# Three first blocks computed by rows, tile by tile, and turned back; masked scores added before their product

## The chip, the cores and the metric

The kernel runs on one core of one Trainium2 chip, as one launch. The metric is the device time of one execution in microseconds. The program keeps five engines busy, each with its own queue that it works off in order: TensorE (PE, matmuls and transposes, its weight loads shown as PEld), VectorE (DVE), ScalarE (ACT), GpSimd (POOL) and the queue that issues most DMAs (SP). They wait for one another by semaphores only.

## What is computed

256 tokens of 1024 values pass through two blocks, in float32. Cut to what the change touches:

```python
def mixer(h, ...):                              # first block: convolution half and gated linear attention half
    ...
    o_f = gla_chunked(qh, kh, vh, af)           # forward; chunks of 64 tokens
    o_b = flip(gla_chunked(flip(qh), flip(kh), flip(vh), flip(ab)))
    o = o_f + o_b                               # in each: where(mask, scores, 0) @ v  +  q_in @ state
    ...
def conv_mlp(h, w_up, conv_w, w_down):
    u = dwconv3(h @ w_up, conv_w)               # width-3 convolution over tokens, 2 x 2816 columns
    gate, val = jnp.split(u, 2, axis=-1)
    return (jax.nn.silu(gate) * val) @ w_down
def first_block(x, ...):
    x = x + rmsnorm(mixer(rmsnorm(x, g0), ...) , g1)
    x = x + rmsnorm(conv_mlp(rmsnorm(x, g2), ...), g3)
def second_block(x, ...):                       # i = 0: fox + stick-breaking attention, then swiglu; i = 1: windows, experts
    x = layer_norm(ALPHA * x + fox_sb_mixer(x, w_in, b_f, w_out), ...)
    x = layer_norm(ALPHA * x + swiglu(x, w_gate_up, w_down), ...)
    x = x + sigmoid(x @ w_ple_gate) * (p @ w_ple_proj)
```

## The kernel before

Tokens lie in two tiles of 128 (t = 0, 1). Every large matrix product is made of float32r matmuls in three parts: high part of the operand by high part of the weights, high by low, low by high. Weights come in chunks of 1 MB (128 x 2048 values: four 128-row slices of 512 columns) through a ring of four slots. For each chunk SP loads `w_raw`, ACT rounds it to `w_hi`, DVE subtracts to get `w_lo` (`split_chunk`), and PE uses both. Chunks are numbered through the program: `w_in` has 0 to 12, `w_out` 13 to 16, `w_up` begins at 17. SP may load into a slot when DVE is done with the low part of its last chunk, ACT may round when PE is done with it. A block of 512 output columns takes two chunks.

The order is written out by hand for each engine; `round_to(c)` on ACT and DVE means "round (split) all chunks below c now", and everything behind it in that engine's program waits for it.

A block is computed in one of two shapes. By rows (`rows_chunk`): the tokens are the stationary side, the weights stream 512 wide, and the result has tokens on the partitions; one block is 2 tiles x 8 slices x 3 parts = 48 matmuls. By columns (`cols_chunk`, `products_t`): the weights are stationary, both token tiles stream 256 wide, and the result has columns on the partitions, as the convolution over tokens, the attention's keys and the next product need it; one block is 96 matmuls.

Ahead of a product, a norm ends tile by tile on DVE (`rms_before`, `normalize`, which add to `t_source`). PE transposes the tile (`turn_tile`, eight 128x128 transposes into PSUM banks 4 to 7, called `scr`), ACT rounds the result to `xt_hi` (`turned`), DVE makes `xt_lo` (`turned`). In `operand` PE does this for both tiles, with matmuls of no use (`keep_warm`) between, and the first block by columns starts when both tiles' high parts are there.

The change touches four places. In order of time: the masked scores `st` of the linear attention (two directions, each multiplied by v on PE); the seam from `w_out` to `w_up` (operand 2); from `w_down` to `ab_in` (operand 3); from `ab_out` to `ffn_up` (operand 5). The two up projections consist of pairs of blocks, gate and value, which PE runs in a loop of five trips (`split_loop`, `up`) while ACT and DVE have the same trips written out.

Of the kernel before, what the change touches and what calls it, by code (L numbers as in the profile page):

```python
# [14 lines left out]
ALU = mybir.AluOpType  # L15
# [101 lines left out]
def build(nc, a, out, upto="end"):  # L117
# [27 lines left out]
    with ExitStack() as ctx:  # L145
# [129 lines left out]
        scr = psum[:, 4:8, :]  # L275

# [375 lines left out]
        def _(act):  # L652
# [108 lines left out]

            act.dma_start(gain[:, 0, :], a["norm_mix_pre"][0:1, :].broadcast_to([P, D])).then_inc(S("first_gain"), 16)
# [68 lines left out]
            for t in range(NT):  # L831
                square_x(t, y, lambda t: act.wait_ge(S("x_tile"), t + 1))
                root_tile(t)
            for j in range(2):
                turned(2, j)


            def up_conv(blocks, r):
# [4 lines left out]
                def middle_tap(h, u, bb):  # L843
                    for k in range(nc_):
                        ch = h * KF + 4 * j + k
                        i = copy(u[:, k, :], acc_t(bb % 2, k), scale=cw[:, 1, ch:ch + 1])
# [86 lines left out]
            if "ab_in" in live:  # L933
# [5 lines left out]
                turned_block(ks_b, ks_t)  # L939
# [28 lines left out]
            if "ab_out" in live:  # L968
                pace("ab_out")
                root_tile(0)  # L970
                turned(5, 0)
                root_tile(1)

            def up_gated(blocks, r):
# [3 lines left out]
                wait_used(act, cv)  # L978
                if j:
                    act.wait_ge(S("h_ready"), KP + j)  # L980
                copy(ug[:, 0:nc_, :], acc_tall(bg % 2, nc_), ACT.Silu).then_inc(S(f"acc_free{bg % 2}"), 1)
# [8 lines left out]
            if "ffn_up" in live:  # L990
                for j in range(1, 4):
# [215 lines left out]
        def _(dve):  # L1207
# [15 lines left out]

            def turned(m, j, n=1):
# [51 lines left out]
            def rms_after(i, name, done):  # L1276
# [8 lines left out]
                round_to(c1 + len(p1_) + 2)  # L1285
# [36 lines left out]
            def follow_norm(name, i, between=None):  # L1322
# [7 lines left out]
                round_to(c1 + len(p1_) + 2)  # L1330
                for t in range(NT):
# [6 lines left out]
                    normalize(t, i, x)  # L1338
                dve.sem_inc(S("gain_used"), 2)
# [73 lines left out]
            round_to(13)  # L1413
            wait_used(dve, gb_b[1] + len(gb_b[4]))
# [53 lines left out]
            def up_conv(blocks, r):  # L1468
# [3 lines left out]
                def outer_taps(h, u, bb):  # L1472
                    dve.wait_ge(S("tap_mid"), 2 * j + h + 1)
                    for tap in (0, 2):
                        o, s = (slice(1, SEQ), slice(0, SEQ - 1)) if tap == 0 else (slice(0, SEQ - 1), slice(1, SEQ))
                        for k in range(nc_):
                            ch = h * KF + 4 * j + k
                            STT(u[:, k, o], acc_t(bb % 2, k)[:, s], cw[:, tap, ch:ch + 1], u[:, k, o], ALU.mult, ALU.add)
                        dve.drain()
                    dve.sem_inc(S(f"acc_free{bb % 2}"), 1)  # L1480

                round_to(cv + 2)
# [18 lines left out]
            if "w_up" in live:  # L1501
                dve.wait_ge(S("cw_turned"), 1)
                spare = 2 * (phase["w_out"][0][0] % 2)
                dve.tensor_copy(cw[:].rearrange("p j k -> p (j k)"), psum[:, spare, 0:3 * 2 * KF]).then_inc(S("cw_ready"), 1)
                operand(2)
# [165 lines left out]
            if "ab_out" in live:  # L1671
                follow_norm("ab_out", 4)

            def up_gated(blocks, r):
# [3 lines left out]
                wait_evacuated(dve, bg)  # L1678
# [11 lines left out]
            if "ffn_up" in live:  # L1690
                operand(5)
# [380 lines left out]
        def _(pe):  # L2072
# [40 lines left out]

            def wait_acc(bb, r=0):
# [245 lines left out]
            pe.wait_ge(S("state_ready"), 1)  # L2360
            for t in range(NT):
# [33 lines left out]
            rows_chunk(out_b[0], 1, yh, yl)  # L2395
            last_rows("w_out", yh, yl)


            def up(blocks, r, m=2):
# [533 lines left out]
```

## Time and profile before

| | |
|---|---|
| three runs | 1809.41, 1809.52, 1811.39 us (median 1809.52) |
| profiled execution, own time | 1811.62 us |
| its span, first to last instruction | 1809.9 us |
| PE busy | 1777.9 us, 98% of the span |
| DVE, ACT, POOL busy | 1373.5, 1099.0, 69.8 us |
| mean granted clock of PE | 0.995 of full speed |

A profile gives for every instruction its engine, its line in the program, its start and how long it took. The busy share of PE counts matmuls of no use as well, so it alone does not say how much of the span is needed. The timeline shows instructions in order of time; in brackets stands how long the engine had been idle before, and whose event ended that. "DVEq" is DVE's sequencer, here the signal that follows a drain. Matmuls overlap: each lasts longer than the distance to the next one, so a stretch is read from starts to starts.

### The profile page before, as it was taken

Reading aid. Unit: us, or ns where it says so; the run is one execution under the profiler, and the core shown is the slowest. Engines: PE = TensorE matmul, PEld = TensorE weight load, DVE = VectorE, ACT = ScalarE, POOL = GpSimd, SP = SyncE. Lnnn points to the kernel's source line nnn. Section 1 sums busy time; section 2 is a strip of 40 time slices with the busy share of each in tenths; the row PEclk is TensorE's granted clock in tenths of the full one; section 3 lists DMA queues with packets and bytes.
Section 4 is the critical chain, followed back from the end, with each engine's and each line's share of the span. In section 5 each row is a group of like instructions: output and inputs, shape, how many; then the busy total and the mean of one; then the engine's idle time right before and its main releaser. Section 6 shows DMA issues by size and latency. Waiting matters only on the chain.

```text
span 1809.9 us, 23787 instructions
## 1 busy us (share of the span) xinstructions
PE 1777.9 (98%) x9653; PEld 1493.8 (83%) x9660; DVE 1373.5 (76%) x1224; ACT 1099.0 (61%) x976; POOL 69.8 (4%) x95
## 2 busy tenths in 40 slices
PE   8999999999999999999999999999999999999997
PEld 6979998887899877778788888888888888888886
DVE  4766785468655565789988888898888888888986
ACT  5545554374344345376676676767767767777763
POOL 2200000200000001000000000000000000000100
PEclk8999999999999999999999999999999999999999
DMA  7444556433555553279999999999999999999991
GB/s 261 164 170 152 186 171 224 153 119 122 183 183 185 184 195 139 71 261 382 333 396 375 344 398 358 368 389 338 392 386 340 399 354 365 395 354 380 403 347 62
DMA packets 250470, 496.75 MB, mean 274 GB/s; under 512 B 10630, under 2 KB 15818, under 8 KB 250368
## 3 DMA queue, kind: packets, MB, share of 16 engines
q1 hardware_dynamic: 244992, 477.30, 72.8%
q0 software_dynamic: 4944, 16.50, 2.5%
q10 hardware_dynamic: 432, 1.57, 0.2%
q8 instruction: 66, 1.08, 0.2%
q14 instruction: 36, 0.29, 0.0%
HBM read 489.56 MB, written 5.78 MB: 274 GB/s over the span
## 4 chain that ended last, share of the span: by engine, by line
PE 91%; DVE 5%; issue 1%; DVEq 1%; ACT 1%; DMA 0%; ACTq 0%; SPq 0%
PE psum L2784 17%; PE psum L2786 16%; PE psum L2785 16%; PE psum L2089 5%; PE psum L2184 5%; PE psum L2186 5%; PE psum L2187 5%; PE psum L2090 5%; PE psum L2091 5%; PE psum L2207 3%; DVE w_lo L1802 2%; PE psum L2169 1%; PE psum L2165 1%; PE psum L2167 1%; DVE w_lo L1216 1%
## 5 line engine op out<-in xcount | busy, mean ns | idle before, releaser
L658 ACT ACTIVATE w_hi<-w_raw 128x2048 fp32r<-128x2048 f32 (+1 forms) x357 | 641.9, 1835 | 97.3 <-PE psum L2091 57.8
L1802 DVE TENSOR_TENSOR w_lo<-w_raw,w_hi 128x2048 fp32r<-128x2048 f32 (+1 forms) x236 | 506.9, 2187 | 72.7 <-ACT w_hi L658 72.5
L2784 PE MATMUL psum<-w_hi,xg_hi 128*128 128x512 f32 x892 | 356.3, 399 | 1.1 <-DVE w_lo L1802 1.1
L1216 DVE TENSOR_TENSOR w_lo<-w_raw,w_hi 128x2048 fp32r<-128x2048 f32 (+2 forms) x121 | 266.3, 2229 | 114.2 <-ACT w_hi L658 111.9
L2786 PE MATMUL psum<-w_hi,xg_lo 128*128 128x512 f32 x892 | 352.3, 395 | 0.0
L2785 PE MATMUL psum<-w_lo,xg_hi 128*128 128x512 f32 x892 | 352.0, 395 | 0.0
L1802 DVE TENSOR_TENSOR w_lo<-raw_more,w_hi 128x2048 fp32r<-128x2048 f32 (+1 forms) x116 | 250.1, 2195 | 35.6 <-ACT w_hi L658 35.3
L658 ACT ACTIVATE w_hi<-raw_more 128x2048 fp32r<-128x2048 f32 (+1 forms) x118 | 210.6, 1823 | 17.4 <-PE psum L2786 12.8
L2184 PE MATMUL psum<-xt_hi,w_hi 128*128 128x256 f32 (+2 forms) x768 | 217.9, 284 | 0.0
L2186 PE MATMUL psum<-xt_lo,w_hi 128*128 128x256 f32 (+2 forms) x768 | 217.1, 283 | 0.0
L2187 PE MATMUL psum<-xt_hi,w_lo 128*128 128x256 f32 (+2 forms) x768 | 217.1, 283 | 0.0
L2786 PEld LDWEIGHTS psum<-w_hi,xg_lo 128*128 128x128 f32 x892 | 167.8, 188 | 39.7
L2784 PEld LDWEIGHTS psum<-w_hi,xg_hi 128*128 128x128 f32 x892 | 167.9, 188 | 39.6 <-DVE w_lo L1802 2.0
L2785 PEld LDWEIGHTS psum<-w_lo,xg_hi 128*128 128x128 f32 x892 | 168.0, 188 | 37.6
L2784 PE MATMUL psum<-w_hi,mh_hi 128*128 128x512 f32 x448 | 178.2, 398 | 0.5 <-DVE w_lo L1802 0.5
L2786 PE MATMUL psum<-w_hi,mh_lo 128*128 128x512 f32 x448 | 176.9, 395 | 0.0
L2785 PE MATMUL psum<-w_lo,mh_hi 128*128 128x512 f32 x448 | 176.8, 395 | 0.0
L2184 PEld LDWEIGHTS psum<-xt_hi,w_hi 128*128 128x128 f32 (+2 forms) x768 | 143.8, 187 | 1.3 <-issue 0.8
L2186 PEld LDWEIGHTS psum<-xt_lo,w_hi 128*128 128x128 f32 (+2 forms) x768 | 143.8, 187 | 0.5
L2187 PEld LDWEIGHTS psum<-xt_hi,w_lo 128*128 128x128 f32 (+2 forms) x768 | 143.8, 187 | 0.3
L658 ACT ACTIVATE mg<-psum 128x512 f32<-128x512 f32 x56 | 33.5, 598 | 166.6 <-PE psum L2786 166.6
L2784 PEld LDWEIGHTS psum<-w_hi,mh_hi 128*128 128x128 f32 x448 | 84.3, 188 | 20.2 <-issue 1.1
(439 smaller groups left out, 2260.6 us busy)
## 6 DMA issues: line engine op xcount, KB each, us to landing
w_raw<-in_moe_w_gate_up SPq DMA_DIRECT2D x150, 1024.0 KB, 8.9
raw_more<-in_moe_w_gate_up SPq DMA_DIRECT2D x74, 1024.0 KB, 8.7
w_raw<-in_moe_w_down SPq DMA_DIRECT2D x64, 1024.0 KB, 7.1
raw_more<-in_moe_w_down SPq DMA_DIRECT2D x32, 1024.0 KB, 7.0
w_raw<-in_w_up SPq DMA_DIRECT2D x22, 1024.0 KB, 5.2
w_raw<-in_ffn_w_gate_up SPq DMA_DIRECT2D x22, 1024.0 KB, 5.5
w_raw<-in_w_in SPq DMA_DIRECT2D x12, 1024.0 KB, 5.9
w_raw<-in_ab_w_in SPq DMA_DIRECT2D x12, 1024.0 KB, 5.2
```

Of the source, the lines that this page charges most:

```text
L658: return act.activation(o, i, func, **kw)
L1216: TT(w_lo[:, k % RING, 0:n], raw(slot, n), w_hi[:, k % RING, 0:n].bitcast(F32), ALU.subtract)\
L1802: TT(w_lo[:, at, 0:n], raw(slot, n), w_hi[:, at, 0:n].bitcast(F32), ALU.subtract).then_inc(S("lo_ready"), 1)
L2089: mm(o, hi(k, t), wh, start=(k == ps[0][0]), stop=False)
L2090: mm(o, hi(k, t), wl, start=False, stop=False)
L2091: m = mm(o, lo(k, t), wh, start=False, stop=(k == kmax))
L2184: mm(o, w_hi[:, slot, cols], xt_hi[:, k, :], start=(k == 0 and c_ % 2 == 0), stop=False, skip_group_check=True)
L2186: mm(o, w_hi[:, slot, cols], xt_lo[:, k, :], start=False, stop=False, skip_group_check=True)
L2187: m = mm(o, w_lo[:, slot, cols], xt_hi[:, k, :], start=False, stop=(k == KD - 1), skip_group_check=True)
L2784: mm(o, hi[:, q, :], wh, start=(q == first), stop=False)
L2785: mm(o, hi[:, q, :], wl, start=False, stop=False)
L2786: m = mm(o, lo[:, q, :], wh, start=False, stop=(q == last))
```

## The change

On DVE the two masked score tiles are added to one, so that PE multiplies one of them by v. At the three seams the first block (gate of both up projections, the keys of `ab_in`) is computed by rows, tile 0 first, by a new function `rows_by_tile`: all that needs only tile 0 stands ahead of the transposes of tile 1. Its result is copied to SBUF by ACT, transposed back by PE after half of the next block (`turned_gate`), and taken from there. The useless matmuls at these seams are gone. DVE and ACT interleave the norms of the two tiles with the halves of a low part (`split_half`) and with tile 0's operand. PE's loop over the pairs of the up projections is written out. Cut to its core:

```diff
+        uv_rows = uv[:].rearrange("p k n -> p (k n)").rearrange("p (t n) -> p t n", n=NB)
+        ks_rows = vs
+        turned_gate = scr[:, 0:2, :].rearrange("p b (f n) -> p (b f) n", n=SEQ)
 # ACT
+            def first_gate(block_):
+                wait_used(act, cc + len(ps))
+                for t in range(NT):
+                    i = copy(uv_rows[:, t, :], acc[bb % 2][t])
+                i.then_inc(S(f"acc_free{bb % 2}"), 1)
             for t in squares("w_out"):
                 root_tile(t)
-            for t in range(NT):
+                if t == 1:
+                    turned(2, 0)
+                    turned(2, 1)
                 square_x(t, y, lambda t: act.wait_ge(S("x_tile"), t + 1))
                 root_tile(t)
-            for j in range(2):
-                turned(2, j)
...
                 round_to(cv + 2)
-                wait_used(act, cv)
                 if j == 0:
+                    first_gate(blocks[0])
+                    round_to(cv + 3)
                     act.wait_ge(S("cw_ready"), 1)
+                    act.wait_ge(S("up_turned"), 2)
+                else:
+                    wait_used(act, cv)
                 middle_tap(0, ug, bg)
 # DVE
+            def split_half(h):
+                k, o = me.chunk, slice(h * (CHUNK // 2), (h + 1) * (CHUNK // 2))
+                dve.wait_ge(S("hi_ready"), k + 1)
+                i = TT(w_lo[:, k % RING, o], w_raw[:, k % RING, o], w_hi[:, k % RING, o].bitcast(F32), ALU.subtract)
+                if h:
+                    dve.drain().then_inc(S("lo_ready"), 1)
+                    me.chunk += 1
             round_to(13)
+            dve.drain()
+            TT(st[:, 0], st[:, 0], st[:, 1], ALU.add).then_inc(S("st_ready"), 1)
-            for t in rms_after(1, "w_out", "x_tile"):
-                pass
-            for t in range(NT):
-                rms_before(t, 2)
+            for t in rms_after(1, "w_out", "x_tile", 1, conv_taps):
+                if t == 0:
+                    split_half(0)
+                    rms_before(0, 2)
+                else:
+                    turned(2, 0)
+                    turned(2, 1)
+                    rms_before(1, 2)
+                    split_half(1)
 # follow_norm("ab_out", 4, first_rows, halves=True)
-                round_to(c1 + len(p1_) + 2)
+                round_to(c1 + len(p1_) + (1 if halves else 2))
...
                     normalize(t, i, x)
+                    if halves:
+                        split_half(t)
 # PE
+            def rows_by_tile(bl, m_, src, between=None):
...
+                high(0, 0)
+                high(1, 0)
+                low_weights(0, 0)
+                low_rows(0, 0)
+                low_rows(1, 0)
+                turn_tile(m_, src, 1)
+                if between:
+                    between()
+                low_weights(1, 0, True)
+                high(0, 1)
+                high(1, 1)
+                low_weights(0, 1)
+                low_rows(0, 1).then_inc(S("w_used"), 1)
+                low_weights(1, 1)
+                low_rows(1, 1, True).then_inc(S("w_used"), 1)
-                        for d in range(2):
-                            mm(o[u], st[:, d, u, pair * NT + t, :], p0[:, t, O_V + h * HEAD_V:O_V + (h + 1) * HEAD_V],
-                               start=(d == 0), stop=False)
+                        mm(o[u], st[:, 0, u, pair * NT + t, :], p0[:, t, O_V + h * HEAD_V:O_V + (h + 1) * HEAD_V],
+                           start=True, stop=False)
+            def up_first(name, m_, src, between=None):
+                gate_b, val_b = phase[name][0:2]
+                turn_tile(m_, src, 0)
+                wait_acc(gate_b[0])
+                rows_by_tile(gate_b, m_, src, between)
...
+                wait_acc(val_b[0])
+                cols_chunk(val_b, 0)
+                wait_evacuated(pe, gate_b[0])
+                for k in range(4):
+                    for t in range(NT):
+                        i = turn(turned_gate[:, k, t * P:(t + 1) * P], uv_rows[:, t, k * P:(k + 1) * P])
+                i.then_inc(S("up_turned"), 1)
+                cols_chunk(val_b, 1)
+                for b_ in phase[name][2:]:
+                    products_t(b_, 0)
-                operand(3, x)
-                products_t(ks_b, 0, 3)
-                products_t(qs_b, 0)
+                turn_tile(3, x, 0)
+                wait_acc(ks_b[0])
+                rows_by_tile(ks_b, 3, x)
+                wait_acc(qs_b[0])
+                cols_chunk(qs_b, 0)
...
+                cols_chunk(qs_b, 1)
```

In `rows_by_tile`, `high(i, t)` is chunk i by tile t with both high parts, `low_weights` high operand by low weights, `low_rows` low operand by high weights: four matmuls each. The three small transposes of the convolution's taps (`cw_rows`) move from the seam to the middle of `w_out`.

PE at the seam from `w_out` to `w_up`, before: the taps' transposes (`cw_rows`), both tiles of `y` turned with useless matmuls (`ones_tri`) around them, then the loop over blocks by columns.

```order
L2412 MATMUL psum<-ident,cw_rows 128x44 x3
L2212 MATMUL psum<-ones_tri 128x512 x8
L2207 MATMUL psum<-ident,y 128x128 x8
L2212 MATMUL psum<-ones_tri 128x512 x5
L2207 MATMUL psum<-ident,y 128x128 x8
L2212 MATMUL psum<-ones_tri 128x512 x2
L371 UNCONDITIONAL_BRANCH
L371 ISA
L2153 ISA
L2167 MATMUL psum<-xt_hi,w_hi 128x256
L2169 MATMUL psum<-xt_hi,w_lo 128x256
```

The same place now.

```order
L2310 MATMUL psum<-ident,y 128x128 x8
L2184 MATMUL psum<-w_hi,xt_hi 128x512 x8
L2184 MATMUL psum<-w_lo,xt_hi 128x512 x4
L2184 MATMUL psum<-w_hi,xt_lo 128x512 x8
L2310 MATMUL psum<-ident,y 128x128 x8
L2184 MATMUL psum<-w_lo,xt_hi 128x512 x4
L2184 MATMUL psum<-w_hi,xt_hi 128x512 x8
L2184 MATMUL psum<-w_lo,xt_hi 128x512 x4
L2184 MATMUL psum<-w_hi,xt_lo 128x512 x4
L2184 MATMUL psum<-w_lo,xt_hi 128x512 x4
L2184 MATMUL psum<-w_hi,xt_lo 128x512 x4
L2287 MATMUL psum<-xt_hi,w_hi 128x256
```

Twenty of the block's 48 matmuls now stand between the transposes of tile 0 and those of tile 1, and the 15 useless ones are gone.

DVE at the same seam, before: two low parts of weights, then the second norm of `w_out` for tile 0 (`stat`, `y`, `x`) and tile 1, and only then the norm that makes the operand `y`.

```order
L1216 TENSOR_TENSOR w_lo<-w_raw,w_hi 128x2048 x2
L1288 TENSOR_TENSOR stat<-stat 128x1
L1265 TENSOR_SCALAR stat<-stat 128x1
L1292 TENSOR_TENSOR y<-psum,gain 128x512
L1256 RECIPROCAL stat<-stat 128x1
L1296 SCALAR_TENSOR_TENSOR x<-y,stat,x 128x1024
L1288 TENSOR_TENSOR stat<-stat 128x1
L1265 TENSOR_SCALAR stat<-stat 128x1
L1292 TENSOR_TENSOR y<-psum,gain 128x512
L1256 RECIPROCAL stat<-stat 128x1
L1296 SCALAR_TENSOR_TENSOR x<-y,stat,x 128x1024
L1265 TENSOR_SCALAR stat<-stat 128x1
```

The same place now.

```order
L1245 TENSOR_TENSOR w_lo<-w_raw,w_hi 128x2048
L1328 TENSOR_TENSOR stat<-stat 128x1
L1303 TENSOR_SCALAR stat<-stat 128x1
L1332 TENSOR_TENSOR y<-psum,gain 128x512
L1294 RECIPROCAL stat<-stat 128x1
L1336 SCALAR_TENSOR_TENSOR x<-y,stat,x 128x1024
L1257 TENSOR_TENSOR w_lo<-w_raw,w_hi 128x1024
L1303 TENSOR_SCALAR stat<-stat 128x1
L1294 RECIPROCAL stat<-stat 128x1
L1311 SCALAR_TENSOR_TENSOR y<-x,stat,gain 128x1024
L1328 TENSOR_TENSOR stat<-stat 128x1
L1303 TENSOR_SCALAR stat<-stat 128x1
```

One of the two low parts is split in halves and put behind tile 0's `x`, and tile 0's operand is made before tile 1's second norm begins.

## Rows read from the trace of the kernel before

**Rows 1.** The page's first line

```profile
span 1809.9 us, 23787 instructions
```

**Rows 2.** Timeline, `w_out` to `w_up`: start us, length us, engine, line, instruction [idle before]

```profile
122.80 0.40 PE L2089 MATMUL psum<-w_hi,ya_hi 128*128 128x512 f32 x1
...
125.40 0.15 DVE L1288 TENSOR_TENSOR stat<-stat 128x1 f32<-128x1 f32 x1
...
128.18 0.40 PE L2091 MATMUL psum<-w_hi,xt_lo 128*128 128x512 f32 x1
...
129.35 0.16 DVE L1288 TENSOR_TENSOR stat<-stat 128x1 f32<-128x1 f32 x1 [1.32 <-ACTq L723]
...
132.21 0.15 DVE L1265 TENSOR_SCALAR stat<-stat 128x1 f32<-128x1 f32 x1 [0.22 <-issue]
...
134.27 1.09 PE L2207 MATMUL psum<-ident,y 128*128 128x128 f32 x8 [3.56 <-DVEq L1274]
...
139.07 0.47 PE L2167 MATMUL psum<-xt_hi,w_hi 128*128 128x256 f32 x1
```

**Rows 3.** Windows: us, length, busy us of five engines, granted clock, DMA share, GB/s

```profile
135.00:136.00 1.00, 1.00 (x7) 0.54 (x6) 0.99 (x1) 1.00 (x2) 0.00 (x0) 0.74 0.50 164
136.00:137.00 1.00, 1.00 (x3) 0.38 (x2) 0.79 (x3) 0.05 (x1) 0.29 (x1) 0.50 0.00 0
...
138.00:139.00 1.00, 1.00 (x6) 0.84 (x5) 0.23 (x1) 0.60 (x2) 0.00 (x0) 0.55 0.87 340
```

**Rows 4.** Timeline, `w_down` to `ab_in`

```profile
328.83 1.07 ACT L658 ACTIVATE xt_hi<-psum 128x512 fp32r<-128x512 f32 x2
...
344.09 1.03 ACT L658 ACTIVATE ks_t<-psum 128x1024 f32<-128x1024 f32 x1 [7.72 <-PE psum L2187]
```

**Rows 5.** Timeline, `ab_out` to `ffn_up`

```profile
447.43 4.49 DVE L1216 TENSOR_TENSOR w_lo<-w_raw,w_hi 128x2048 fp32r<-128x2048 f32 x2
...
451.84 0.68 DVE L1304 SCALAR_TENSOR_TENSOR x<-x,psum 128x512 f32<-128x512 f32 x1
...
454.34 0.40 PE L2091 MATMUL psum<-w_hi,xt_lo 128*128 128x512 f32 x1
...
456.74 1.09 PE L2207 MATMUL psum<-ident,x 128*128 128x128 f32 x8 [2.00 <-DVEq L1320]
...
461.85 1.09 PE L2207 MATMUL psum<-ident,x 128*128 128x128 f32 x8 [1.21 <-DVEq L1320]
461.98 2.48 DVE L1228 TENSOR_TENSOR xt_lo<-psum,xt_hi 128x512 fp32r<-128x512 f32 x4 [0.21 <-issue]
...
475.24 1.03 ACT L658 ACTIVATE ug<-psum 128x1024 f32<-128x1024 f32 x1 [5.89 <-PE psum L2187]
```

**Rows 6.** Chain of waits that ended last: start us, us on the chain, what

```profile
91.91 0.89 PE psum L2368 x8
...
93.67 1.09 PE psum L2368 x8
...
108.10 0.87 PE psum L2207 x8
```

**Rows 7.** Timeline, DVE beside the linear attention's products

```profile
85.57 1.22 DVE L1416 TENSOR_TENSOR gct<-gct,psum 128x1024 f32<-128x1024 f32 x1 [1.96 <-POOL gct L560]
...
91.03 1.23 DVE L1434 TENSOR_TENSOR ya_lo<-gct,ya_hi 128x1024 fp32r<-128x1024 f32 x1 [0.21 <-issue]
```

**Rows 8.** Window of 192 matmuls by columns in `w_up`, over a trip's end (162.3)

```profile
143.27:166.31 23.04, 23.04 (x194) 23.04 (x194) 12.67 (x18) 11.02 (x13) 0.00 (x0) 1.00 0.55 183
```

**Rows 9.** Timeline, ACT and DVE behind the first gate block of `w_up`

```profile
150.98 1.57 ACT L658 ACTIVATE ug<-psum,cw 128x256 f32<-128x256 f32 x4 [7.78 <-PE psum L2187]
...
159.31 2.29 DVE L1216 TENSOR_TENSOR w_lo<-w_raw,w_hi 128x2048 fp32r<-128x2048 f32 x1 [0.83 <-ACT w_hi L658]
164.11 3.39 DVE L1478 SCALAR_TENSOR_TENSOR uv<-psum,cw,uv 128x255 f32<-128x255 f32 x8 [2.51 <-ACT uv L658]
...
168.97 2.29 DVE L1216 TENSOR_TENSOR w_lo<-w_raw,w_hi 128x2048 fp32r<-128x2048 f32 x1
```

More of the change, by code:

```diff
@@ L971, in _ @@
                 turned(5, 0)
+                turned(5, 1)
                 root_tile(1)
@@ L990, in _ @@
             if "ffn_up" in live:
-                for j in range(1, 4):
+                for j in range(2, 4):
                     turned(5, j)
@@ L1274, in rms_before, with rms_after @@
                 dve.drain().then_inc(S("t_source"), 2)
-            def rms_after(i, name, done):
+            def rms_after(i, name, done, ahead=2, between=None):
                 (b0, c0, _, _, p0_), (b1, c1, _, _, p1_) = phase[name]
@@ L1284, in rms_after @@
                 dve.drain().then_inc(S(f"acc_free{b0 % 2}"), 1)
[L1285 removed]
+                if between:
+                    between()
+                round_to(c1 + len(p1_) + ahead)
                 for t in range(NT):
@@ L1472, in outer_taps @@
                 def outer_taps(h, u, bb):
+                    first = h == 0 and j == 0
                     dve.wait_ge(S("tap_mid"), 2 * j + h + 1)
@@ L1477, in outer_taps @@
                             ch = h * KF + 4 * j + k
-                            STT(u[:, k, o], acc_t(bb % 2, k)[:, s], cw[:, tap, ch:ch + 1], u[:, k, o], ALU.mult, ALU.add)
+                            src = turned_gate[:, k, s] if first else acc_t(bb % 2, k)[:, s]
+                            STT(u[:, k, o], src, cw[:, tap, ch:ch + 1], u[:, k, o], ALU.mult, ALU.add)
                         dve.drain()
-                    dve.sem_inc(S(f"acc_free{bb % 2}"), 1)
-                round_to(cv + 2)
+                    if not first:
+                        dve.sem_inc(S(f"acc_free{bb % 2}"), 1)
+                round_to(cv + (2 if j else 3))
                 outer_taps(0, ug, bg)
@@ L1501, in _ @@
             if "w_up" in live:
[L1502 to L1505, printed above, removed]
+                for j in range(2, 4):
+                    turned(2, j)
                 split_loop(dve, "w_up", up_conv, me, unroll=True)
@@ L1671, in _, with first_rows @@
             if "ab_out" in live:
-                follow_norm("ab_out", 4)
+                def first_rows():
+                    if "ffn_up" in live:
+                        turned(5, 0)
+                        turned(5, 1)
+                follow_norm("ab_out", 4, first_rows, halves=True)
             def up_gated(blocks, r):
@@ L1690, in _ @@
             if "ffn_up" in live:
-                operand(5)
+                for j in range(2, 4):
+                    turned(5, j)
                 split_p(0)
@@ L2112, in rows_operand_high_first, with part, high, low_weights @@
                 m.then_inc(S("w_used"), 1)
+            def rows_by_tile(bl, m_, src, between=None):
+                bb, cc, n0, n, ps = bl
+                def part(i, t, of, w, last=False):
+                    for k in range(4 * i, 4 * i + 4):
+                        j = mm(acc[bb % 2][t][:, 0:n], of(k, t), w[:, (cc + i) % RING, (k - 4 * i) * n:(k - 4 * i + 1) * n],
+                               start=(k == 0 and of is xh and w is w_hi), stop=(last and k == 4 * i + 3))
+                    return j
+                def high(i, t):
+                    pe.wait_ge(S("hi_ready"), cc + i + 1)
+                    pe.wait_ge(S("xt_hi_ready"), 4 * m_ + 2 * t + i + 1)
+                    part(i, t, xh, w_hi)
+                def low_weights(i, t, last=False):
+                    pe.wait_ge(S("lo_ready"), RING + cc + i + 1)
+                    return part(i, t, xh, w_lo, last)
+                def low_rows(i, t, last=False):
+                    pe.wait_ge(S("xt_ready"), 4 * m_ + 2 * t + i + 1)
+                    return part(i, t, xl, w_hi, last)
+                high(0, 0)
[4 more added lines that the diff above has]
+                turn_tile(m_, src, 1)
+                if between:
+                    between()
+                low_weights(1, 0, True)
[5 more added lines that the diff above has]
+                low_rows(1, 1, True).then_inc(S("w_used"), 1)
             def wait_acc(bb, r=0):
@@ L2572, in _ @@
             if "ffn_up" in live:
-                operand(5, x)
-                turn_p(0)
-                split_loop(pe, "ffn_up", lambda blocks, r: up(blocks, r, 5))
+                up_first("ffn_up", 5, x, lambda: turn_p(0))
             if "ffn_down" in live:
```

60 lines of the change are left out of this document (39 added, 21 removed).

## The prediction, as it was put on record

> **What bounds the kernel now.** I read the page first, then PE's waits, then the timeline around each of the four places. PE is busy for nearly the whole span [rows 1], so a change gains time only where PE waits for something or does work that is not needed; DVE and ACT count only where PE waits for them. The waits named the seams, and the timeline shows what is in them. Between `w_out` and `w_up`, PE issues its last useful matmul at 128.18 and its next at 139.07 [rows 2]: nearly 11 us, of which 16 transposes are needed. It stands still for 3.56 of that, then the granted clock falls to half, the 1.2 GHz level, for about three microseconds [rows 3]. At `ab_out` to `ffn_up`, PE waits 2.00 and 1.21 around the two tiles, with useless matmuls between [rows 5]. In the linear attention the products with `st` come in four groups, 0.89 on the chain for the first and 1.09 for each of the other three [rows 6], and PE waits for nothing there.
>
> **The change part by part.** I carry each place forward on the clock of before, as if the places ahead of it had gained nothing, and add up. A matmul by rows costs (128.18 - 122.80) / 23 = 0.234 us from start to start [rows 2], so a block by rows is 48 x 0.234 = 11.2. By columns 192 take 23.04 [rows 8]: 0.12 each, 5.8 for half a block, 11.5 for a block. The end of a first block I read from the ACT copy that waits for it: 150.98, 344.09 and 475.24 [rows 9, 4, 5]. It trails the last issue by about 0.35 (139.07 + 11.5 against 150.98).
>
> *Masked scores.* Half of 0.89 + 3 x 1.09 goes: 2.1 us. The new addition on DVE is 1024 wide, 1.23 by its nearest row [rows 7]. It stands where DVE was idle for 1.96 until 85.57 waiting for POOL, with a drain before it; the products start at 91.9. Without this cover it would cost at most 1.4 on DVE, and since PE and the chain behind it both start from these products, all that follows moves by the same 2.1.
>
> *`w_out` to `w_up`, until the gate block ends.* The taps' three transposes now stand on PE's path, 0.35 (eight larger ones take 0.87 [rows 6]). Tile 0 of `w_out` is last issued at 122.57, now 122.9. For tile 1 the statistic follows the last issue by 129.35 - 128.18 = 1.17; for tile 0 before it came only at 125.40, because DVE was in the second of two low parts. With one of them put later the statistic comes at 124.1. From there to the finished x is under 132.21 - 129.35 = 2.86, less 0.22 idle: 126.75. Now ACT squares x while nothing hides it: 1.03, as its other 1024-wide copies take, and 0.3 for reading the sum and the hand-over: 128.1. DVE uses this time for half a low part (1.23). From the scalar step to the transposes are 134.27 - 132.21 = 2.06: tile 0 is turned at 130.3, and PE, done at 128.75, waits 1.5. The first rounded half is there 1.3 later (estimate: 0.5 for four transposes, half of 1.03 on ACT, two hand-overs): real matmuls start at 131.6 instead of 139.07. Twenty of them last to 136.3. Meanwhile DVE takes tile 1: statistic 130.2, x 132.85, square 134.2, transposes possible at 136.4. PE waits 0.1, transposes 1.0, waits perhaps 0.3 for the second half of the low part (136.35 + 1.23), and does the other 28: 144.4, with the trail 144.75, against 150.98. That is 6.2.
>
> *`w_down` to `ab_in`.* DVE and ACT do here what they did. The first rounded half is there at 328.83 + half of 1.07, so PE starts at 329.4; tile 1 has long been normalised when PE gets to it. 329.4 + 11.2 + 1.0 for the transposes + 0.35 = 341.95 against 344.09: 2.2.
>
> *`ab_out` to `ffn_up`.* DVE splits one chunk less ahead of tile 0 (4.49 / 2 = 2.25 at 447.43), so tile 0's add moves from 451.84 to 449.6 and its transposes from 456.74 to 454.5, when PE is just done (454.34). Real matmuls start 1.3 later, at 455.95; twenty last to 460.65. On DVE tile 1 follows tile 0 by 461.85 - 456.74 = 5.1, and now has half a low part (1.23) and two of the four low operand pieces (2.48 / 2) in front: 462.1. PE waits 1.4, turns tile 1 and the four blocks of p (1.6), does 28 more: 470.2, with the trail 470.6 against 475.24: 4.7.
>
> *Turned back.* Eight transposes, 0.87 [rows 6], three times: 2.6 lost. The ACT copies to SBUF before them end within half a block by columns (5.8), which hides them.
>
> *The first pair of `w_up`.* Everything ACT does for the gate now starts from the transposes back, half a block later against PE than before. From ACT's first tap to the low part of chunk 22 are 159.31 + 2.29 - 150.98 = 10.6; PE needs it two half blocks after the transposes, 11.5: just in time. The outer taps of the value block then start right behind it instead of at 164.11, and from them to the low part of chunk 23 are 168.97 + 2.29 - 164.11 = 7.15: in all 17.9 from ACT's start, 18.1 from the transposes. PE needs it after 3 half blocks, 17.3: a new wait of 0.8 that stands nowhere before. Behind this low part on DVE are chunk 24 and the next taps; by the same rows both are early by 1.5 or more, so it occurs once. Bounds: 0 to 2. In `ffn_up` the gate needs one ACT instruction instead of taps, and the same sum leaves some 6 us of room.
>
> *PE's loops written out.* I put this at nothing: over a trip's end PE is busy 23.04 of 23.04 us, so no branch costs anything now [rows 8]. The Trainium skill says otherwise in "Runtime: NRT & Kernel Launch", section "Instruction fetch mechanics": instructions are fetched ahead in sequence only, and a taken branch to code outside the fetched pages stalls until its page has come. By that rule writing out eight trip ends would give something on top; the trace does not show a stall, and the sum takes nothing for it.
>
> Sum: 2.1 + 6.2 + 2.2 + 4.7 - 2.6 - 0.8 = 11.8. The profiled execution would go from a span of 1809.9 to 1798.1; its own time, 1811.6, lies 2.1 above the median of the runs, 1809.5, from which I take the same 11.8: **1797.7 us**. What I could not read from the trace are the hand-overs in the new order (bounds: 1.5 each way at the two long seams), the new wait (0 to 2) and the clock (below). With these the case itself reaches from 1795 to 1801.
>
> **Rivals.**
>
> *The clock falls.* The useless matmuls are gone, and PE now waits 1.5, does 1 us of transposes and waits again before the real work. Before, a wait of 3.56 with 8 transposes behind it was followed by half clock [rows 2, 3]. Against it: after a wait of 2.00 the eight transposes took 1.09 like elsewhere [rows 5], and no wait of mine is longer. One fall costs 0.26 + 0.50 + 0.50 + 0.45 = 1.7 us of PE's work at full speed; at the two long seams and `ab_in` up to 5. The time: 1799.5 to 1803.
>
> *Tile 1 is late.* PE's queue holds 28 matmuls, the value block and all else behind the transposes of tile 1. If DVE and ACT get in each other's way there (ACT takes tile 0's rounding between tile 1's root and its square, DVE two pieces of the operand between), the wait is not 0.1 and 1.4 but 3 to 4 at each long seam, and half of the gain is left: about 1803. For it speaks that four hand-overs in a row are new; against it that each of them was laid out above from a measured one.
>
> *The written-out PE code comes too slowly.* 8 blocks of each up projection, 1536 matmuls in all, become straight code. If that code came slower than PE eats it, each would be longer than 0.12. From 11.8 / 1536 = 0.008 on, 6% more, the change is slower than before; at 0.014 the time is 1819. Against it: the blocks of `w_out` are written out and run evenly at 0.234 for a matmul twice as wide, and those of `ab_in` are written out by columns and leave PE no gap.
>
> *It does not do what it says.* If a wait in `rows_by_tile` covers both tiles after all, only masked scores and the missing useless matmuls count: 1804 to 1807.
>
> **How the numbers follow.** My case 0.70; clock 0.12; late tile 1 0.11; not what it says 0.03; slow code 0.04. The range from 1794 to 1803.5 holds the first two and most of the third. What a measurement of this kernel can tell from no change is 0.2%, 3.6 us, so faster means below 1805.9. All of the first three cases and half of the fourth do: 0.94. Same: 0.03; slower: 0.03.
>
> **What would show it.** In the trace of the changed kernel: the `st` group with half its matmuls and about 0.5 long; at `w_up` the first 512-wide matmul some 3 us behind the last of `w_out`, a wait under 0.5 ahead of tile 1, and the ACT copy of the gate 6 us earlier; at `ab_in` 2 us earlier; at `ffn_up` no wait ahead of tile 0 and 1 to 2 us ahead of tile 1. One PE wait of about 0.8 for a low part of weights, in the second value block of `w_up`. A granted clock of 1.00 throughout the seams. I am wrong if the clock falls at a seam, if PE waits over 2.5 for tile 1, if the wait for the low part comes back in later pairs, or if matmuls by columns in the up projections are further apart than 0.121.

## The result, and the profile after

The changed kernel takes 1796.87 us (median; 1796.84 to 1798.10), the kernel before, timed beside it, 1809.47: a ratio of 0.993, 95% interval 0.9912 to 0.9947. Forecast were 1797.7 us and a range of 1794 to 1803.5. The profiled executions took 1811.62 and 1798.10 us. The page's first line, beside the one of before [rows 1]:

```profile
span 1796.4 us, 23383 instructions
```

PE at the three seams, timeline of the changed kernel (start us, length us, engine, line, instruction, idle before and what ended it). L2310 is a transpose, L2184 a matmul by rows.

```profile
128.20 1.09 PE L2310 MATMUL psum<-ident,y 128*128 128x128 f32 x8 [1.15 <-DVEq L1312]
129.63 2.10 PE L2184 MATMUL psum<-w_hi,xt_hi 128*128 128x512 f32 x8 [0.34 <-ACT xt_hi L662]
...
134.37 1.04 PE L2310 MATMUL psum<-ident,y 128*128 128x128 f32 x8
135.60 1.20 PE L2184 MATMUL psum<-w_lo,xt_hi 128*128 128x512 f32 x4 [0.19 <-DVEq L1259]
...
321.54 2.11 PE L2184 MATMUL psum<-w_hi,xt_hi 128*128 128x512 f32 x8 [1.19 <-ACT xt_hi L662]
...
445.23 1.05 PE L2310 MATMUL psum<-ident,x 128*128 128x128 f32 x8
446.62 2.10 PE L2184 MATMUL psum<-w_hi,xt_hi 128*128 128x512 f32 x8 [0.34 <-ACT xt_hi L662]
...
452.67 1.09 PE L2310 MATMUL psum<-ident,x 128*128 128x128 f32 x8 [1.15 <-DVEq L1360]
```

Between `w_out` and `w_up` the first real matmul is issued at 129.63, where before it was at 139.07 [rows 2]; tile 1's transposes at 134.37 wait for nothing. At `ffn_up` tile 0 does not wait, tile 1 waits 1.15. The waits of 3.56, 2.00 and 1.21 before [rows 2, 5] are gone; the longest at the three seams is now the 1.19 of `ab_in`.

Windows of the changed kernel over the same two seams (us, length, busy us of PE, PEld, DVE, ACT, POOL, granted clock, DMA share, GB/s):

```profile
126.00:130.00 4.00, 2.51 (x15) 1.72 (x14) 3.22 (x9) 2.25 (x7) 0.00 (x0) 1.00 0.00 0
130.00:134.00 4.00, 4.00 (x19) 3.26 (x18) 3.50 (x6) 1.35 (x3) 0.00 (x0) 1.00 0.00 0
134.00:138.00 4.00, 3.81 (x21) 2.99 (x20) 2.77 (x5) 2.99 (x4) 1.07 (x2) 1.00 0.25 46
...
448.00:456.00 8.00, 6.85 (x37) 5.42 (x36) 7.30 (x11) 2.84 (x5) 1.64 (x3) 1.00 0.10 19
```

The granted clock is 1.00 throughout, the 2.4 GHz level (in both traces of the changed kernel, and without a break from 20 to 1756 us), where before it was 0.50 for some three microseconds [rows 3].

Beside the short waits at the seams, one wait of PE is new in the changed kernel, and it comes once (waiter, what it waited for: us in total, times, longest):

```profile
PE psum L2287 <- DVE w_lo L1245: 0.7, 1, 0.7
```

**Two pairs of executions.** The two spans of the profiled executions differ by 13.5 us, the medians by 12.6. Both kernels were profiled once more (experiments 11 and 12): spans of 1807.6 and 1795.6, 12.0 apart. The marks of that second pair follow; each mark is the same work in both kernels. The kernel before:

```profile
90.73 1.05 PE L2368 MATMUL psum<-p,st 128*128 128x128 f32 x8
98.57 1.02 ACT L658 ACTIVATE e<-psum 128x1024 f32<-128x1024 f32 x1 [8.00 <-PE psum L2374]
149.99 1.57 ACT L658 ACTIVATE ug<-psum,cw 128x256 f32<-128x256 f32 x4 [7.72 <-PE psum L2187]
321.07 0.58 ACT L658 ACTIVATE psum<-psum 128x512 f32<-128x512 f32 x1 [2.21 <-PE psum L2091]
341.81 1.03 ACT L658 ACTIVATE ks_t<-psum 128x1024 f32<-128x1024 f32 x1 [7.71 <-PE psum L2187]
353.20 1.03 ACT L658 ACTIVATE qs_t<-psum 128x1024 f32<-128x1024 f32 x1 [6.76 <-PE psum L2187]
473.19 1.03 ACT L658 ACTIVATE ug<-psum 128x1024 f32<-128x1024 f32 x1 [5.89 <-PE psum L2187]
484.71 1.22 DVE L1681 TENSOR_TENSOR uv<-ug,psum 128x1024 f32<-128x1024 f32 x1 [4.17 <-PE psum L2187]
```

The changed kernel (its first blocks are copied to `uv` and `vs`):

```profile
91.42 0.61 PE L2471 MATMUL psum<-p,st 128*128 128x128 f32 x4
97.47 1.02 ACT L662 ACTIVATE e<-psum 128x1024 f32<-128x1024 f32 x1 [5.33 <-PE psum L2477]
142.34 1.09 ACT L662 ACTIVATE uv<-psum 128x512 f32<-128x512 f32 x2 [2.75 <-PE psum L2184]
315.28 0.58 ACT L662 ACTIVATE psum<-psum 128x512 f32<-128x512 f32 x1 [2.21 <-PE psum L2155]
333.79 1.09 ACT L662 ACTIVATE vs<-psum 128x512 f32<-128x512 f32 x2 [2.26 <-PE psum L2184]
346.05 1.02 ACT L662 ACTIVATE qs_t<-psum 128x1024 f32<-128x1024 f32 x1 [2.87 <-PE psum L2290]
460.78 1.09 ACT L662 ACTIVATE uv<-psum 128x512 f32<-128x512 f32 x2 [2.30 <-PE psum L2184]
473.24 1.22 DVE L1744 TENSOR_TENSOR uv<-ug,psum 128x1024 f32<-128x1024 f32 x1 [0.69 <-PE psum L2290]
```

Subtract each mark of after from the one of before (-0.69, 1.10, 7.65, 5.79, 8.02, 7.15, 12.41, 11.47); the step from one difference to the next is what the stretch between gained. The first difference is scatter: over the fourteen traces the products with `st` start at 90.1 to 91.8, whatever the kernel.

| stretch, up to | predicted | first pair | second pair |
|---|---|---|---|
| the linear attention's result is read | 2.1 | 1.79 | 1.79 |
| the first gate block of `w_up` is read | 6.2 | 6.54 | 6.55 |
| the end of `w_down` (turned back, new wait) | -1.7 | -0.56 | -1.86 |
| the keys of `ab_in` | 2.2 | 2.22 | 2.23 |
| the queries of `ab_in` (turned back) | -0.9 | -0.87 | -0.87 |
| the gate block of `ffn_up` | 4.7 | 5.05 | 5.26 |
| the first value block of `ffn_up` (turned back) | -0.9 | -0.87 | -0.94 |
| sum | 11.8 | 13.3 | 12.2 |

At the gate block of `ffn_up` the second pair has 0.2 more than the first: in the second trace of the kernel before the clock fell at this seam, too, in the first it did not.

### The profile page after: what moved, and what is told of

It is laid out like the page before. It is cut to its first block, busy times and chain, and to the rows that moved or that the text cites. A ratio compares the mean times of both kernels' runs of the same rounds, so it can differ in the third digit from the quotient of the medians.

```text
span 1796.4 us, 23383 instructions
## 1 busy us (share of the span) xinstructions
PE 1766.9 (98%) x9479; PEld 1482.2 (83%) x9483; DVE 1377.1 (77%) x1227; ACT 1101.7 (61%) x982; POOL 75.1 (4%) x95
## 4 chain that ended last, share of the span: by engine, by line
PE 90%; DVE 6%; issue 1%; ACT 1%; DVEq 1%; DMA 0%; ACTq 0%; SPq 0%
PE psum L2901 17%; PE psum L2903 17%; PE psum L2902 17%; PE psum L2287 6%; PE psum L2290 5%; PE psum L2289 5%; PE psum L2153 5%; PE psum L2155 5%; PE psum L2154 5%; PE psum L2310 3%; DVE w_lo L1866 1%; PE psum L2184 1%; DVE w_lo L1245 1%; DMA w_raw<-in_w_in 0%; DVE x L1357 0%
## 5 line engine op out<-in xcount | busy, mean ns | idle before, releaser
L1245 DVE TENSOR_TENSOR w_lo<-w_raw,w_hi 128x2048 fp32r<-128x2048 f32 (+3 forms) x119 | 262.3, 2230 | 111.9 <-ACT w_hi L662 109.8
L2287 PE MATMUL psum<-xt_hi,w_hi 128*128 128x256 f32 (+2 forms) x880 | 249.1, 283 | 0.7 <-DVE w_lo L1245 0.7
L2290 PE MATMUL psum<-xt_hi,w_lo 128*128 128x256 f32 (+2 forms) x880 | 248.0, 282 | 0.0
L2289 PE MATMUL psum<-xt_lo,w_hi 128*128 128x256 f32 (+2 forms) x880 | 248.0, 282 | 0.0
L662 ACT ACTIVATE w_hi<-raw_more 128x2048 fp32r<-128x2048 f32 (+1 forms) x118 | 210.5, 1824 | 16.1 <-PE psum L2903 12.6
L2287 PEld LDWEIGHTS psum<-xt_hi,w_hi 128*128 128x128 f32 (+2 forms) x880 | 164.5, 187 | 2.4 <-issue 1.7
L2289 PEld LDWEIGHTS psum<-xt_lo,w_hi 128*128 128x128 f32 (+2 forms) x880 | 164.5, 187 | 0.6
L2290 PEld LDWEIGHTS psum<-xt_hi,w_lo 128*128 128x128 f32 (+2 forms) x880 | 164.4, 187 | 0.3
```

Of the source, the lines that this page charges most:

```text
L662: return act.activation(o, i, func, **kw)
L1245: TT(w_lo[:, k % RING, 0:n], raw(slot, n), w_hi[:, k % RING, 0:n].bitcast(F32), ALU.subtract)\
L2287: mm(o, w_hi[:, slot, cols], xt_hi[:, k, :], start=(k == 0 and c_ % 2 == 0), stop=False, skip_group_check=True)
L2289: mm(o, w_hi[:, slot, cols], xt_lo[:, k, :], start=False, stop=False, skip_group_check=True)
L2290: m = mm(o, w_lo[:, slot, cols], xt_hi[:, k, :], start=False, stop=(k == KD - 1), skip_group_check=True)
```

## The experiments

All are timed beside the kernel before, which took 1809.3 to 1810.0 in the median. The question left by the first pair was the third row: 1.1 us too good. In its traces matmuls by columns stand 0.1200 us apart, from start to start, in `w_up` before [rows 8], 0.1187 after, and the change writes PE's loop there out.

**1, the loop written out in the kernel before.**

```diff
-                split_loop(pe, "w_up", up)
+                split_loop(pe, "w_up", up, unroll=True)
```

(and the same for `ffn_up`)

> The kernel before with PE's trips of both up projections written out, nothing else. In the changed kernel the matmuls by columns of w_up stand 0.1187 us apart, 0.1200 before; over the 1056 of w_up that is about 1.3 us that the prediction did not have. Theory A (the loop costs nothing, as predicted; 0.1200 has another cause): 1809.5, w_up still at 0.1200. Theory B (the loop code slows it): 1808.2, w_up at 0.1187.

Measured: 1809.84 against 1809.34, ratio 1.0001 (0.9992 to 1.0011). The time is theory A's, but the distance in `w_up` is 0.1187: neither theory has both.

**5, the loop put back in the changed kernel.**

```diff
-                for b_ in phase[name][2:]:
-                    products_t(b_, 0)
+                trips, bl = LOOPS[name][0] - 1, phase[name][2:]
+                with pe.Fori(0, trips) as r:
+                    for b_ in bl[0:2]:
+                        products_t(b_, r)
...
```

> The changed kernel with PE's trips 2 to 5 of both up projections in a loop again (the first pair stays written out). Theory A (the loop costs nothing): 1796.9, w_up at 0.1187. Theory B (the loop makes 0.1200 in w_up): 768 matmuls x 0.0013 = 1.0 more, 1797.9.

Measured: 1797.32 (1796.93 to 1798.76) and 0.1187 in `w_up` from 150 us on (0.1193 to 0.1198 in the 8 us before). The loop costs nothing to speak of and does not make the distance.

**11 and 12, both kernels unchanged, profiled again.**

> The kernel before, unchanged, in another profiled execution. Theory A (the distance of 0.1200 between matmuls by columns of w_up in the first trace is a property of that execution, since the same loop ran at 0.1187 in two of the experiments): 0.1187 here is possible, w_up then 1.4 shorter. Theory B (it belongs to this kernel, by what stands ahead of w_up): 0.1200 again. Time 1808.5 to 1812 either way.

> The changed kernel, unchanged, in another profiled execution. Theory A: 0.1187 or 0.1200 in w_up, the rest of each seam within 0.1 of the first trace. Theory B: 0.1187 again. Time 1796.8 to 1798.2.

Measured: 1809.34 and 1797.33. The first matmul by columns of `w_up` and the first matmul of `w_down` in the second trace of before:

```profile
138.32 0.36 PE L2167 MATMUL psum<-xt_hi,w_hi 128*128 128x256 f32 x1
...
263.71 0.39 PE L2089 MATMUL psum<-w_hi,ht_hi 128*128 128x512 f32 x1
```

and the latter in its first trace, which answers to 139.07 [rows 2]:

```profile
265.98 0.39 PE L2089 MATMUL psum<-w_hi,ht_hi 128*128 128x512 f32 x1
```

Between the two lie 125.39 us here, 126.91 in the first trace of the same program; experiments 1, 2 and 3 have 125.51, 125.39 and 125.39. So the 0.1200 belonged to the one execution that was profiled first, and some 1.5 us of the first pair's 13.5 are not the change's.

**2, the masked scores alone, in the kernel before.**

```diff
+            dve.drain()
+            TT(st[:, 0], st[:, 0], st[:, 1], ALU.add).then_inc(S("st_ready"), 1)
...
-                        for d in range(2):
-                            mm(o[u], st[:, d, u, pair * NT + t, :], ...
+                        mm(o[u], st[:, 0, u, pair * NT + t, :], ...
```

> The kernel before with the masked scores added on DVE and multiplied once, nothing else. Prediction: 2.1 us less, 1807.4. By the trace of the changed kernel the copy that follows is 1.8 earlier: 1807.7. Rival (the addition on DVE makes something else late, or w_out takes the gain back at its wait for weights): 1809 or more.

Measured: 1807.61 against 1809.34, ratio 0.9988 (0.9978 to 0.9998). From the products to the copy of their result are 6.05 us (90.37 to 96.42) against 7.84 before: 1.79 again, and the medians agree. Its ten executions spread from 1805.2 to 1810.1, and with the granted clock: three at a mean of 0.997 took 1805.2 to 1805.6, seven at 0.994 or 0.995 took 1807.2 to 1810.1. In the profiled one, of the former, the clock stayed at 1.00 between `w_out` and `w_up`, and from tile 0's transposes to the first matmul by columns are 3.53 us, against 4.80 in the first trace of before.

**3, the kernel before without useless matmuls at the seams.**

```diff
-            BEFORE = (0, 10, 8, 0, 18, 0, 4, 0, 18, 0, 24)
-            BETWEEN = (0, 4, 5, 9, 4, 13, 4, 2, 4, 11, 4)
+            BEFORE = (0, 10, 0, 0, 18, 0, 4, 0, 18, 0, 24)
+            BETWEEN = (0, 4, 0, 0, 4, 0, 4, 2, 4, 11, 4)
...
+                if m not in (2, 3, 5):
                     keep_warm(2, 3)
```

> The kernel before without the useless matmuls at the three seams (operands 2, 3 and 5), nothing else. Theory A (they only fill waits): 1809.5, within 0.6. Theory B (without them the clock stays at half for longer behind the seams): up to 3 us more, with windows of granted clock below 1.00 that last beyond the first matmuls by columns. Theory C (w_up runs at 0.1200 because it is entered behind useless matmuls at half clock): 0.1187 in w_up and 1808.2.

Measured: 1813.13 against 1809.34, ratio 1.002 (1.001 to 1.003): theory B, 3.8 for a bound of 3. Windows of its trace at `ab_out` to `ffn_up`, columns as above:

```profile
454.00:456.00 2.00, 1.11 (x5) 1.11 (x6) 1.80 (x3) 0.00 (x0) 0.00 (x0) 0.74 0.64 232
456.00:460.00 4.00, 0.85 (x4) 0.45 (x3) 3.40 (x6) 1.28 (x3) 0.00 (x0) 0.50 0.00 0
460.00:464.00 4.00, 4.00 (x19) 4.00 (x20) 3.18 (x5) 2.33 (x4) 1.82 (x3) 0.50 0.57 198
464.00:466.00 2.00, 2.00 (x14) 2.00 (x14) 0.90 (x2) 2.00 (x2) 0.00 (x0) 0.70 0.77 256
```

PE waits, 2.00 ahead of tile 0 and 3.15 ahead of tile 1 with only transposes between, the clock goes to 0.50, the 1.2 GHz level, and stays there into the block: 19 matmuls and transposes in 4 us, where later windows have 19 in 2. The same is seen at `w_up` (0.50 from 131 to 137). So the useless matmuls paid for themselves before, and the clock rival was no idle fear: the changed kernel leaves them out too. How much of the 3.8 falls at the seams, the traces tell: from the first product with `st` to the first matmul of `ffn_down` are 498.10 here and 496.18 in the second trace of before, 1.9 more, within the bound. Another 2.0 lie far behind, where the code is the same: there the clock is at 0.50 from 1779.5 to 1786 here, from 1768.6 to 1771.9 in that trace of before. Whether the edit has to do with that is not shown. Why does the changed kernel's clock hold?

**4, the changed kernel with both tiles turned first.**

```diff
+                turn_tile(m_, src, 1)
                 high(0, 0)
                 high(1, 0)
                 low_weights(0, 0)
                 low_rows(0, 0)
                 low_rows(1, 0)
-                turn_tile(m_, src, 1)
```

> The changed kernel with tile 1 turned ahead of the whole first block at all three seams, so that no real matmul stands between the tiles. Theory A (the gain of the two long seams is that twenty matmuls of tile 0 lie beside tile 1's norm): each long seam loses 20 x 0.233 = 4.7, ab_in gains up to 1.0 (its 1.19 wait is covered by the second tile's transposes), together 8.4 more than 1796.9: 1805.3; and, since PE then waits with nothing between the tiles, the clock falls as it did without useless matmuls (experiment before this), which adds 1 to 4: 1805 to 1810. Theory B (the order of the tiles does not matter, the gain is the missing useless matmuls): within 1 of 1796.9.

Measured: 1811.65, ratio to before 1.0011 (1.0002 to 1.002): 14.8 lost, the whole gain and more. Its waits (columns as above):

```profile
PE psum L2310 <- DVEq L1360: 6.5, 1, 6.5
PE psum L2310 <- DVEq L1312: 6.2, 2, 5.1
PE psum L2310 <- DVEq L1337: 2.7, 1, 2.7
```

and the clock at `w_up`:

```profile
128.00:132.00 4.00, 0.00 (x0) 0.00 (x0) 3.42 (x8) 1.92 (x5) 0.00 (x0) 0.62 0.00 0
132.00:134.00 2.00, 1.06 (x5) 1.09 (x6) 1.88 (x2) 0.00 (x0) 0.00 (x0) 0.50 0.00 0
134.00:136.00 2.00, 2.00 (x9) 1.77 (x8) 1.25 (x3) 1.68 (x3) 1.07 (x2) 0.56 0.40 45
```

Theory A, but worse than its range, and my expectation for `ab_in` was wrong: tile 1 is not there in time, PE waits 2.7 for its norm. From tile 0's transposes to the first matmul by columns this kernel needs 19.54, 17.26 and 21.71 us at the three seams, the changed one 14.02, 14.34 and 15.40: 14.7 together.

**10, the same with the waits covered by useless matmuls.**

```diff
+                keep_warm({2: 18, 3: 9, 5: 24}[m_])
                 turn_tile(m_, src, 1)
                 high(0, 0)
```

> The kernel with both tiles turned first (1811.7) and useless matmuls between the tiles: 18, 9 and 24 of them at the three seams, 0.22 us each, just shorter than its waits of 5.06, 2.72 and 6.47 there. Theory A (that kernel lost 10.8 by the order and some 4 more because the clock fell behind the uncovered waits): the clock stays at 1.00 at the seams, 1807 to 1808.5. Theory B (the clock costs nothing here, all is the order): 1811.7. Theory C (useless matmuls delay tile 1): above 1812.

Measured: 1807.52 (1806.44 to 1808.10), ratio 0.9989 (0.998 to 0.9999). Windows at `w_up` and `ffn_up`:

```profile
130.00:134.00 4.00, 2.92 (x16) 1.31 (x14) 3.38 (x7) 1.35 (x3) 0.00 (x0) 1.00 0.00 0
...
454.00:458.00 4.00, 2.79 (x14) 1.21 (x13) 3.52 (x7) 0.20 (x1) 0.00 (x0) 1.00 0.00 0
```

Theory A. With cover the clock holds, the three stretches take 18.13, 15.75 and 19.97, and 4.1 us come back by the medians, 4.7 by the three stretches. Of the 14.8 that experiment 4 lost, 4 to 5 were clock and some 10 the order itself. In the changed kernel the twenty real matmuls of tile 0 do both: they fill the wait with work that has to be done, and the clock is held.

**9, `ab_in` by columns in the changed kernel.**

```diff
-                turn_tile(3, x, 0)
-                wait_acc(ks_b[0])
-                rows_by_tile(ks_b, 3, x)
...
+                operand(3, x)
+                products_t(ks_b, 0, 3)
+                products_t(qs_b, 0)
```

> The changed kernel with the seam from w_down to ab_in as before: both tiles turned with useless matmuls between, the keys by columns, no turning back. The prediction's terms for this seam are 2.2 less 0.9: 1.3 more than 1796.9, 1798.2. Rival (the seam gave nothing, and what the trace shows as 2.2 is taken back behind it): 1796.9, within 0.4.

Measured: 1799.17 (1797.41 to 1799.50). In the traces the stretch from the first matmul of `w_down` to tile 0's transposes at `ffn_up` is 188.64 here and 187.26 in the changed kernel: 1.38, the predicted size. The two profiled executions differ by 1.40 as a whole (1799.50 against 1798.10). The medians differ by 2.3; what the other 0.9 is stays open, the four times being 2.1 apart themselves.

**6, chunk 22 rounded earlier in the changed kernel.** Its new wait of 0.7 ends a chain in which DVE stands idle 3.23 us for ACT:

```profile
157.26 2.29 DVE L1245 TENSOR_TENSOR w_lo<-w_raw,w_hi 128x2048 fp32r<-128x2048 f32 x1 [3.23 <-ACT w_hi L662]
```

```diff
                 round_to(cv + 3)
+                if j == 0:
+                    round_to(end + 2)
                 act.wait_ge(S("gate_conv"), j + 1)
```

> The changed kernel with one move on ScalarE: in the first pair of w_up chunk 22 is rounded ahead of the silu of the gate, not behind it. In the trace of the changed kernel VectorE stands idle 3.23 for it, and PE's new wait of 0.73 for chunk 23 is the end of that chain. Theory A (the wait is the late start of the gate's taps, as predicted, and this idle time is where it can be taken out): wait gone, 0.7 less, 1796.2. Theory B (the chain is held by the taps themselves): wait stays, 1796.9.

Measured: 1796.25 (1795.25 to 1796.43); no wait of PE for `w_lo` is left at `w_up`, and DVE, timeline:

```profile
153.30 2.29 DVE L1247 TENSOR_TENSOR w_lo<-w_raw,w_hi 128x2048 fp32r<-128x2048 f32 x1
156.01 3.39 DVE L1537 SCALAR_TENSOR_TENSOR uv<-psum,cw,uv 128x255 f32<-128x255 f32 x8 [0.42 <-ACT uv L662]
```

Theory A: 0.6 less by the medians; from the first matmul by columns of `w_up` to the first matmul of `w_down` are 114.87 us, against 115.76 in the changed kernel, 0.9 less.

**7, the half low part behind tile 1's norm at `ffn_up`.**

```diff
-                    if halves:
-                        split_half(t)
+                    if halves and t:
+                        split_half(0)
+                        split_half(1)
...
-                low_weights(1, 0, True)
+                if m_ != 5:
+                    low_weights(1, 0, True)
                 high(0, 1)
                 high(1, 1)
+                if m_ == 5:
+                    low_weights(1, 0, True)
```

> The changed kernel, at ab_out to ffn_up alone: both halves of the split low part stand behind tile 1's norm on VectorE, and PE multiplies by that low part after tile 1's high parts. Theory A (the wait of 1.15 ahead of tile 1 is the half low part of 1.23 in front of tile 1's norm): wait gone, 1.1 less, 1795.8. Theory B (it only moves the wait to the low part): 0.2 less at most, with a wait of about 1 for the low part.

Measured: 1795.89 (1795.49 to 1796.38). Of the wait of 1.15 ahead of tile 1 this is left:

```profile
PE psum L2314 <- DVEq L1360: 0.2, 1, 0.2
```

and no new one for the low part: theory A, 1.0 less by the medians. From tile 0's transposes to the first matmul by columns are 14.54 here and 15.40 in the changed kernel, 0.9 less. The stretches say more than the medians here: most executions of experiments 6 and 7 have a mean clock of 0.997, the changed kernel 0.996, and in the trace of 7 the clock is at 1.00 from 1757 to 1760, where it is at 0.50 in that of the changed kernel.

**8, both, and `ab_in`'s first tile rounded before tile 1's root.**

```diff
                 for t in squares("w_down"):
+                    if t == 1 and "ab_in" in live:
+                        turned(3, 0)
+                        turned(3, 1)
                     root_tile(t)
```

(DVE's two `turned(3, ...)` move likewise behind tile 0 of `rms_after`; the edits of 6 and 7 are in.)

> The two moves before together, and at w_down to ab_in tile 0's operand is rounded ahead of tile 1's root (its wait of 1.19 on PE is for the rounded half, which stands behind that root on ScalarE). If the three waits are independent: 0.7 + 1.1 + 0.5 = 2.3 less, 1794.6, faster than both kernels. If one of them only moves on: 1795 to 1796.

Measured: 1793.62 (1793.26 to 1795.96), ratio to before 0.9913 (0.9899 to 0.9926). Each of its five times is below each of the changed kernel's (1796.8 to 1798.1), so this version beats both. What is left of its waits:

```profile
PE psum L2193 <- ACT xt_hi L662: 1.4, 3, 0.7
PE psum L2322 <- DVEq L1317: 1.2, 1, 1.2
```

In its trace the three stretches are 114.87 for 115.76, 13.85 for 14.34 and 14.55 for 15.40: 2.2 together, for 2.3 expected, so the three waits are independent. That the medians differ by 3.2 goes with three executions at a mean clock of 0.998 (1793.3 to 1793.6; the two at 0.996 took 1795.2 and 1796.0). Where those three save it wasn't traced.

## Why the prediction was right

*Masked scores.* Right, 1.8 for 2.1 in three traces. A group with half its matmuls now takes 0.53 to 0.64 of PE's time, not half of 0.89 and 1.09 [rows 6].

*`w_out` to `w_up`.* Right, 6.5 for 6.2. The chain ran as laid out, some 2 us earlier in the program's time by then: tile 0 waited 1.15 (forecast 1.5), the first rounded half 0.34, tile 1 nothing (0.1), the half low part 0.19 (0.3). The first matmul by rows stands 9.44 earlier than the first by columns before; 2.0 of that come from what lies ahead of the seam. Of the 6.5, about 1.3 is the half clock that the kernel before lost here: in experiment 2, whose clock stayed at 1.00, the same code took 3.53 for 4.80.

*Turned back.* Right to 0.1: 0.87 and 0.9 where they stand alone.

*The new wait.* Right in place, size and number: 0.73 for 0.8, once, for the low part in the second value block. Experiment 6 shows that the gate's late start was not all of its cause: ACT's order left DVE idle, and the wait could be had for nothing.

*`w_down` to `ab_in`.* The size is right, 2.2, and experiment 9 bears out the net. The premise that tile 1 is long normalised when PE gets to it held, by 3.4 us:

```profile
321.60 1.28 DVE L1336 SCALAR_TENSOR_TENSOR x<-y,stat,x 128x1024 f32<-128x1024 f32 x1
...
326.27 1.04 PE L2310 MATMUL psum<-ident,x 128*128 128x128 f32 x8
```

It holds only because the twenty matmuls stand in front, as experiment 4 showed with its wait of 2.7.

*`ab_out` to `ffn_up`.* Right, 5.05 and 5.26 for 4.7. Tile 0 waits 0, tile 1 1.15 (forecast 1.4).

*Loops written out.* Right at nothing (experiments 1 and 5). The rule of the Trainium skill that was weighed against it ("Runtime: NRT & Kernel Launch", section "Instruction fetch mechanics") would give something on top if the start of a trip lay outside the fetched pages, which no run shows; in these runs a loop of PE's with trips of 192 matmuls costs nothing that can be seen.

*The clock.* Right that it did not fall, but the argument given for it does not hold. The prediction took a wait of 2.00 for harmless, because in its trace the eight transposes behind that wait took 1.09 [rows 5]. In the second trace of the same kernel they take 1.97, and the granted clock is 0.50 from 455 to 457:

```profile
454.47 1.97 PE L2207 MATMUL psum<-ident,x 128*128 128x128 f32 x8 [2.00 <-DVEq L1320]
```

It fell at this seam in experiments 1 and 3 as well, behind the same wait. That it held in the trace that the prediction was read from was chance, and the argument with it. What the runs show in its place: experiment 4 takes the twenty matmuls from between the tiles, PE waits 5.1, 2.7 and 6.5, and the clock falls at all three seams; experiment 10 fills these waits, and it holds. In the changed kernel real work stands there and no wait at a seam is over 1.19. Whether the short waits or the amount of work between them decides is not told apart by any run. The Trainium skill's "TensorE: Matmul & The Clock Gate", section "HAM oscillation — how this bites in real kernels", tells of a clock that falls at waits with little work between them, and regroups the work so that more of it stands between two. Experiments 4 and 10 agree that such waits cost clock: 4.1 us at three seams.

That the first two spans differ by 13.5 and not by 11.8 comes from the trace that the prediction was read from: it held an execution in which `w_up` ran 1.5 us longer than usual. Each term of the sum is a difference of marks on either side of one seam, so this hardly entered it. Two of its steps are off as written: those of `w_up` add up to 144.25 and not 144.4, and 344.09 less 341.95 is 2.14 and not 2.2; together that is 0.1.

## What to carry to other kernels

Where a norm hands tiles to a long product, look for a block of that product that can be computed tile by tile: its first tile's matmuls fill the wait for the second, and the clock holds, which useless matmuls can do, too, but without doing any of the work. Work of another engine that stands in front of a hand-over and is not needed by it (a low part, a root, a silu) is worth moving even by one place: three such moves gave another 2.2 us in the trace. And before a remainder of a microsecond is explained, profile the same program twice.

## What the runs showed of the hardware

Matmuls by columns (256 wide, float32r) run in two rhythms at the granted clock of 1.00: 0.1200 or 0.1187 us apart. One rhythm holds over long stretches (127 us of `w_up` at 0.1200 in the first trace) and the other may be met in the next execution of the same program. In `w_in` both occur within 20 us, and the switch is at transposes or other short matmuls between two runs of columns. What chooses the rhythm stays open; it is worth 1.5 us in `w_up`.

Whether the clock falls at one seam differs between executions of the same code, too. Between `w_out` and `w_up` the kernel before was at 0.50 in both its traces, and with only the scores changed at 1.00, behind the same wait. Between `ab_out` and `ffn_up` it stayed at 1.00 in its first trace and was at 0.50 in its second. That may be why its times spread over 5 us (1808.3 to 1813.2 in 25 executions); those of the changed kernel lie within 1.3, but are only four.
